# Who adds up the squares: TensorE's sums by ones against VectorE's additions, in a two-layer transformer kernel

## The reference, cut to what matters

```python
def rms_norm_2(x, g):
    xf = x.astype(jnp.float32)
    y = xf * lax.rsqrt(jnp.mean(xf * xf, axis=-1, keepdims=True) + EPS)
    return (y * g.astype(jnp.float32)).astype(x.dtype)
...
    q = (rms_norm_2(cq, g_cq) @ w_uq).reshape(b, s, MLA_HEADS, MLA_NOPE + MLA_ROPE)
    kv = (rms_norm_2(ckv, g_ckv) @ w_ukv).reshape(b, s, MLA_HEADS, MLA_NOPE + MLA_V)
```

## Time and profile before

| | |
|---|---|
| median of three runs | 2995.4 us (2993.77 to 2995.87) |
| the profiled execution | time 2993.23 us, span 2991.4 us |
| mean granted TensorE clock | 0.987 |
| busy, share of the span | TensorE 96%, weight loads 76%, VectorE 53%, ScalarE 39%, GpSimd 10% |

### The profile page before, as it was taken

One profiled execution on the slowest core, in us unless ns is written; L12 is line 12 of the kernel. 1 busy time (PEld: TensorE's weight loads), 2 busy tenths in 40 slices (PEclk: granted clock), 3 DMA queues, 4 the chain that ended last, 5 costly groups with the idle time before them and its releaser, 6 DMA issues. The chain is left out here.

```text
span 2991.4 us, 36740 instructions
## 1 busy us (share of the span) xinstructions
PE 2862.3 (96%) x14862; PEld 2285.2 (76%) x14862; DVE 1574.2 (53%) x2158; ACT 1173.5 (39%) x1721; POOL 308.1 (10%) x263
## 2 busy tenths in 40 slices
PE   7999999999999999999999999999899999999998
PEld 2889777678878888786687778888676778778886
DVE  3467256675534443568763355443568663544443
ACT  3642444442233342434643343333435643433332
POOL 0020014310001110001200021100002101111100
PEclk9999999999999999999999999999999999999999
DMA  6200210035422222220032122232120132122221
GB/s 248 71 29 1 78 56 29 29 124 183 159 71 99 98 93 92 92 85 29 29 121 91 57 72 97 98 108 99 71 71 15 57 113 71 67 89 98 98 99 57
DMA packets 45556, 250.08 MB, mean 84 GB/s; under 512 B 4960, under 2 KB 7136, under 8 KB 19040
## 3 DMA queue, kind: packets, MB, share of 16 engines
q1 hardware_dynamic: 45408, 248.01, 23.6%
HBM read 245.90 MB, written 2.10 MB: 83 GB/s over the span
## 5 line engine op out<-in xcount | busy, mean ns | idle before, releaser
L263 DVE TENSOR_TENSOR ring_lo<-ring,ring_hi 128x2048 fp32r<-128x2048 f32 x199 | 457.8, 2300 | 651.6 <-ACT ring_hi L256 651.4
L314 PE MATMUL bank<-h_hi,ring_hi 128*128 128x512 f32 x1360 | 545.6, 401 | 18.0 <-PEq L372 8.7
L256 ACT ACTIVATE ring_hi<-ring 128x2048 fp32r<-128x2048 f32 x199 | 379.8, 1909 | 460.2 <-PE bank L314 393.2
L314 PE MATMUL bank<-h_hi,ring_lo 128*128 128x512 f32 x1360 | 532.4, 391 | 0.0
L1616 PE MATMUL bank<-h_hi,ring_hi 128*128 128x512 f32 x960 | 374.2, 390 | 5.6 <-DVE ring_lo L263 5.6
L1619 PE MATMUL bank<-h_lo,ring_hi 128*128 128x512 f32 x960 | 373.5, 389 | 0.0
L1620 PE MATMUL bank<-h_hi,ring_lo 128*128 128x512 f32 x960 | 373.5, 389 | 0.0
L314 PEld LDWEIGHTS bank<-h_hi,ring_hi 128*128 128x128 f32 x1360 | 256.8, 189 | 77.4 <-issue 9.6
L314 PEld LDWEIGHTS bank<-h_hi,ring_lo 128*128 128x128 f32 x1360 | 256.8, 189 | 55.1
L314 PE MATMUL bank<-h_lo,ring_hi 128*128 128x512 f32 x624 | 245.1, 393 | 0.0
L1616 PEld LDWEIGHTS bank<-h_hi,ring_hi 128*128 128x128 f32 x960 | 180.2, 188 | 45.3 <-DVE ring_lo L263 8.2
(11 more groups left out here) (460 smaller groups left out, 4890.2 us busy)
## 6 DMA issues: line engine op xcount, KB each, us to landing
ring<-in_stream SPq DMA_DIRECT2D x201, 1024.0 KB, 4.7
mod_w<-in_stream SPq DMA_DIRECT2D x64, 256.0 KB, 3.3
xT<-in_xT SPq DMA_DIRECT2D x2, 2048.0 KB, 15.2
ring<-in_stream SPq DMA_DIRECT2D x7, 512.0 KB, 4.2
ring<-in_stream SPq DMA_DIRECT2D x10, 256.0 KB, 3.7
const<-in_const SPq DMA_DIRECT2D x1, 2306.5 KB, 15.6
memT<-in_memT SPq DMA_DIRECT2D x2, 1024.0 KB, 5.0
out<-xT SPq DMA_DIRECT2D x8, 256.0 KB, 2.0
```

Source lines behind the costliest of these rows:

```text
L256: nc.scalar.activation(self.slab_hi(slab + j), self.slab(slab + j), ACT.Copy).then_inc(slab_rounded, 1)
L263: nc.vector.tensor_tensor(lower, self.slab(slab + j), self.slab_hi(slab + j).bitcast(F32), ALU.subtract)\
L314: ins = nc.tensor.matmul(out, lhsT, rhs, start=start and w is w_hi and x is x_hi, stop=stop and w is w_lo)
```

## The change

At the latents VectorE adds the squares of each latent into the first one of it (`low_totals`, hooked to its turn 7, before it reads tile 7 out): two additions and one. TensorE makes one sum by ones for each latent, two in place of five.

In the memory's stage VectorE adds squares 1 to 3 into square 0 behind its last new value of x, halves the slab `first_v`, and adds squares 4 to 7 (`add_next`). Each addition is behind a drain of VectorE. TensorE makes one sum in place of eight, ahead of key tile 7. ScalarE's order stays, but square n from the fourth on waits for addition n - 3 in place of a sum, and the buffers are those of `square_place`: 0 for the running total and three in turn for the others.

```diff
@@ tensor @@
-                def next_sums(which):
-                    for n in which:
-                        if n == 0:
-                            pe.wait_ge(post.scale_ready.sem, post.scale_ready.at(1))
-                        pe.wait_ge(post.next_square_ready.sem, post.next_square_ready.at(n + 1))
-                        nc.tensor.matmul(bank[:, 0, :], con("ones"), post.squares[:, n % SQUARES, :], start=n == 0, stop=n == KT - 1)\
-                            .then_inc(post.next_square_summed.sem, 1)
+                def next_sum():
+                    pe.wait_ge(post.scale_ready.sem, post.scale_ready.at(1))
+                    pe.wait_ge(next_added.sem, next_added.at(KT - 1))
+                    nc.tensor.matmul(bank[:, 0, :], con("ones"), post.square_place(0), start=True, stop=True)\
+                        .then_inc(post.next_square_summed.sem, KT)
...
-                for j in range(5):
+                for j in range(KT - 1):
                     key_tile(j)
-                next_sums(range(4))
-                for j in range(5, KT - 1):
-                    key_tile(j)
-                next_sums(range(4, KT))
+                next_sum()
                 key_tile(KT - 1)
@@ scalar @@
                         if n >= SQUARES:
-                            act.wait_ge(post.next_square_summed.sem, post.next_square_summed.at(n - SQUARES + 1))
-                        nc.scalar.activation(post.squares[:, n % SQUARES, :], xT[:, AHEAD[n], :], ACT.Square)\
+                            act.wait_ge(next_added.sem, next_added.at(n - SQUARES + 1))
+                        nc.scalar.activation(post.square_place(n), xT[:, AHEAD[n], :], ACT.Square)\
@@ vector @@
+                def add_next(n):
+                    dve.drain()
+                    dve.wait_ge(post.next_square_ready.sem, post.next_square_ready.at(n + 1))
+                    nc.vector.tensor_tensor(post.square_place(0), post.square_place(0), post.square_place(n), ALU.add)\
+                        .then_inc(next_added.sem, 1)
...
                 new_x(7)
+                for n in range(1, 4):
+                    add_next(n)
                 ws.halve_to(dve, first_v, ws.limit)
+                for n in range(4, KT):
+                    add_next(n)
                 dve.wait_ge(post.next_scale_ready.sem, post.next_scale_ready.at(1))
@@ layer_body, the latents @@
+                    def low_totals(dve):
+                        for lo, hi, _, _ in latents:
+                            for n in range(lo + 1, hi):
+                                dve.wait_ge(low_squared.sem, low_squared.at(n + 1))
+                                if n > lo + 1:
+                                    dve.drain()
+                                last = nc.vector.tensor_tensor(low_square[lo], low_square[lo], low_square[n], ALU.add)
+                            last.then_inc(low_added.sem, 1)
+
                     def low_sums(pe):
-                        for m, (lo, hi, _, _) in enumerate(latents):
-                            for n in range(lo, hi):
-                                pe.wait_ge(low_squared.sem, low_squared.at(n + 1))
-                                last = nc.tensor.matmul(bank[:, 6 + m, :], con("ones"), low_square[n], start=n == lo, stop=n == hi - 1)
-                            last.then_inc(low_summed.sem, 1)
+                        for m, (lo, _, _, _) in enumerate(latents):
+                            pe.wait_ge(low_added.sem, low_added.at(m + 1))
+                            nc.tensor.matmul(bank[:, 6 + m, :], con("ones"), low_square[lo], start=True, stop=True)\
+                                .then_inc(low_summed.sem, 1)
...
+                            ("dve", 4): lambdas, ("dve", 7): low_totals, ("dve", 9): dve_9, ("dve", 10): dve_10, ("dve", 11): dve_11, ("dve", 12): dve_12,
```

More of the change, by code:

```diff
@@ L1860, in mix_and_memory @@
             added = post.added_by_dve
+            next_added = Signal("squares_added", KT - 1)
             def tensor(pe):
@@ L3165, in layer_body @@
                     low_squared = Signal("square_ready", 5)
+                    low_added = Signal("squares_added", 2)
                     low_summed = Signal("square_summed", 2)
@@ L3370, in layer_body @@
                             ("act", 10): first_gelus, ("act", 16): gate_scalar,
-                            ("dve", 4): lambdas, ("dve", 9): dve_9, ("dve", 10): dve_10, ("dve", 11): dve_11, ("dve", 12): dve_12,
+                            ("dve", 4): lambdas, ("dve", 7): low_totals, ("dve", 9): dve_9, ("dve", 10): dve_10, ("dve", 11): dve_11, ("dve", 12): dve_12,
                             ("dve", 16): values_beside}
```

## The result

The changed kernel takes 3007.9 us (median of five runs, 3007.2 to 3009.7) against 2995.4 (2993.8 to 2996.3): 0.46% slower, ratio 1.0046 with a 95% interval of 1.0033 to 1.0059. The forecast was 3002.7 us, with a range to 3007.0. The sign and the place were right, the size was not: 12.5 us in place of 7.3.

The account below looks back on a forecast made before the run. TensorE, 96% busy, was taken to bound the kernel, except VectorE at the end of the memory's stage. Per layer -2.57 + 4.60 + 1.6 = +3.63 us, twice +7.3, gave 3002.7 us, range 2998.0 to 3007.0.

Parts of the forecast that it names:

- The latents' saving and its cover: Latents: five sums become two, three VectorE adds fit in its 4.75 us wait; -2.57 us per layer.
- The three queues: Memory's stage: TensorE, VectorE and ScalarE rebuilt in order; the sum starts at 1562.53, 10.4 us after TensorE ran dry.
- The delay of 4.60 us: Memory's stage: the root and the stage's end come 4.60 us later per layer; bounds 3.4 and 4.9.
- The clock on the path: Memory's sum and key tile 7: half clock after the new rest costs 1.6 us per layer; bounds nothing and 3.7.
- rival 2: Memory's stage: half clock holds over all of the sum and tile 7; +11.5 us, 3006.9; chance 0.1.
- The bound of 3.7 us: Memory's stage: upper bound of the clock's cost per layer, if the whole sum and key tile 7 run at half.
- They all move earlier as one.: Behind the latents: the work hanging on tile 8 moves earlier together, so the saving arrives; -2.57 us per layer.
- The latents' bound of 0: Latents: no gain per layer if the adds come late by as much as they save.
- Rival 1: Memory's stage: the clock does not fall, or not on the path; +4.1 us, 2999.5; chance 0.12.
- Rival 3: Latents: the saving is lost because roots or adds come late; +12.4 us, 3007.8; chance 0.05.
- Rival 4: Memory's stage: additions keep pace, seventh by 1557.9 in place of 1562.5; 2990.3, or down to 2978.3; chance 0.11.

Follow-up runs that it names:

- Experiment 5: The whole change with squares 4 to 6 of the memory's stage in free tiles of hT, so they wait for no addition; 3001.9 us, ratio 1.0022.
- experiment 8: Experiment 5 with all seven additions ahead of the halving of the first value slab; 2995.6 us, ratio 1.0003.
- experiment 3: The whole change with 46 small unread products of the identity in TensorE's rest ahead of the memory's sum; 3002.0 us, ratio 1.0023.
- experiment 2: Only the memory's part of the change, the latents as in the kernel before; 3007.9 us, ratio 1.0046.
- Experiment 10: Only the latents' part, with 12 small products of the identity delaying its two sums and no filling behind `in2`; 2996.1 us, ratio 1.0004.
- experiment 6: Only the latents' part, with 11 small products of the identity filling TensorE's rest at the end of `in2`; 2988.7 us, ratio 0.9978.
- experiment 1: Only the latents' part of the change, the memory's stage as in the kernel before; 2993.9 us, ratio 0.9997.
- experiment 4: The whole change with key tile 7 ahead of TensorE's only sum in the memory's stage; 3000.8 us, ratio 1.0021.
- experiment 7: Experiment 6 with five of the memory's additions on GpSimd and three sums ahead of key tile 7; 2995.0 us, ratio 1.0000.

## Why the prediction was wrong

**The latents' saving and its cover: right.** Three additions end at 1279.37, 2.6 us before the sums, and the sums shrink by the forecast 2.57 us (2.58 measured at the stage's end).

**The three queues: right to a few tenths.** Adds 1 to 3 were forecast from 1552.84 and stand at 1552.69; the rounding at 1555.13 and 1555.06; the halving at 1557.06 and 1556.99; add 4 at 1559.45 and 1559.38; the sum at 1562.53 and 1562.57, in a trace whose rows stand 0.15 us earlier here. Experiment 5 takes out one link, 2.14 us off the rest, and experiment 8 both, 4.34 us, so held square and halving are shown and not only argued. The delay of 4.60 us measured 4.87, just inside its bound of 4.9; 0.19 of the difference is there at the start of the sum.

**The clock on the path: the term that was mis-sized.** I took 1.6 us a layer from the row after the stage's 3.85 us rest; experiment 3 measured 2.75. The half clock stood over 6.0 us, both passes and 19 of tile 7's 24 products, close to rival 2. The bound of 3.7 us held it, but I took the near row's length for a rest nearly three times as long. Nor is it one figure for one rest: behind the same 10.65 us the half clock stood 6.0 us in the changed kernel and 5.1 in experiment 2. Two layers: 2.3 us.

**The step that failed: "They all move earlier as one."** The work did, the clock did not. I priced the clock only where the change made a new rest. At the start of `up_latent` the rest is as old as the kernel, 2.58 us, and cost nothing until it fell 1.8 us earlier: then 1.61 and 1.63 us, 3.2 in all, that stand in no term of mine. The latents' bound of 0 would have covered them, but for another reason, late additions. Experiment 10 puts the rest back in its place against the clock's last change and the cost is gone; experiment 6 fills the rest and the cost is gone too. In the whole change this undid 3.2 of the latents' 5.2 us.

**The bill.** Forecast +7.3 us; with 2.3 for the clock behind the long rest, 3.2 for the clock behind the old one and 0.5 for the chain (4.87 less 4.60, twice) it is +13.3, which is the +13.3 found in the places of the change in the spans. The medians say +12.5. The other 1.4 us of span are the clock in layer 1's attention and the stretch ahead of `in2`, and the profiled execution of before stood 2.2 us under its median.

**The rivals.** Rival 1, no fall of the clock, is what experiment 3 shows for the memory's place; the change itself was closer to rival 2. Rival 3 came out in part, with 3.2 of the latents' 5.2 us lost, though not by late adds or roots; that its +12.4 is nearly the measured +12.5 is luck, since its sum is made of other terms. Rival 4's point was tried in experiment 8: with the sum 4.34 us earlier the loss is gone, and no gain is there, since the clock still falls (two passes in 2.05 us). The rival says that the whole change is even with the seventh addition 2.57 us earlier; by its own terms that is 4.60 - 2.57 = 2.03 us with the clock at full, and 3.63 us with the 1.6 us of clock.

The Trainium skill, "TensorE: Matmul & The Clock Gate", section "Why this matters for your kernels", warns of long gaps only. The trace agrees for 10.65 and 3.85 us; for 2.58 us it shows both outcomes, by the moment.

## What to carry to other kernels

Before work is moved from a busy engine to an idle one, write out whose queue the result now has to pass: here 5.4 us of additions a layer cost 7.6 us a layer, 4.9 by the chain and 2.7 by the half clock behind the rest, since a square waited for an addition and four additions stood behind a halving that waited for ScalarE. A good part of a hand-over is where the receiving engine already waits: three additions in a 2.12 us wait gave 2.6 us of TensorE a layer back; all seven, in the best order tried, cost 2.1 us. And look at the rests that TensorE already has ahead of and behind the edit: an old rest can begin to cost when the work ahead of it gets shorter, and a few small products in it can make a saving real (the 3.2 us lost in `up_latent` here). Last, when two totals are compared to a microsecond, compare their traces stage by stage: a half clock of another length, in a stretch that neither edit touches, is worth as much as the edit.

## What the runs showed of the hardware

- A rest of 2.58 us of TensorE was followed by the full clock in three kernels (before, experiments 2 and 10) and by a stretch at 1.2 GHz in the six with the latents' part ahead of it and neither filling nor delay (the changed kernel, experiments 1, 3, 4, 5 and 8), in 11 of their 12 layers; the one that kept the full clock is layer 2 of experiment 8, so that the moment of the rest decides and not the code: it ended 98.0 to 98.2 us behind the last stretch at the half clock in the eleven, 96.7 and 100.6 to 100.8 us behind it in the others. The eight warming products then take 2.84 to 3.04 us for 2.02.
- At the half clock the 256-column products follow each other every 0.21 us for 0.12, and an fp32 pass of 512 columns takes 1.06 to 1.19 us for 0.59.
- Products of the identity that nobody reads held the clock at full through 10 us (experiment 3).
- GpSimd's additions with both inputs in SBUF slow VectorE's instructions with two SBUF inputs that begin while one of them runs (experiment 7: 1.76 for 0.74 us, 1.67 and 1.01 for 0.69, 3.38 for 2.29). The one instruction a layer that reads PSUM and lies beside an addition takes its usual 0.74 us:

```profile
1539.60 2.36 POOL L1869 TENSOR_TENSOR squares<-squares 128x512 f32<-128x512 f32 x1 [67.29 <-ACT squares L1981]
1540.72 0.74 DVE L2056 SCALAR_TENSOR_TENSOR raw<-bank,par,scales 128x512 f32<-128x512 f32 x1
1541.50 1.01 DVE L2059 TENSOR_TENSOR xT<-xT,raw 128x512 f32<-128x512 f32 x1
```

The Trainium skill, "SBUF — State Buffer", section "Who interferes with whom", says that a VectorE instruction with two SBUF inputs contends with a GpSimd instruction that reads SBUF, and calls the port pair that the two share an exclusive lock. The trace agrees in which instructions are slowed, by 0.32 us and by 0.98 to 1.09, and in the other direction: the addition above began during a halving that kept its 2.29 us, and took 2.36 us itself where another took 1.54. That each delay is the whole of the other instruction is not shown.
